# Weight splits, the turned keys' copies and the end of a feed-forward in another order, in a two-block float32 transformer on one core

## The reference, cut

```python
u = a * jax.nn.sigmoid(b)                 # first mixer: conformer branch
u = causal_depthwise_conv(u, w_dw)        # 31 taps, 256 channels
u = jax.nn.silu(layer_norm(u, ln_g, ln_b)) @ w_pw
log_f = jax.nn.log_sigmoid(f_logit)       # first mixer: forgetting attention
...
q = (rms_norm_2(c_q, q_norm) @ w_uq)      # attention: 8 latent heads of 64 + 32 (rope)
kv = (rms_norm_2(c_kv, kv_norm) @ w_ukv)
o_mla = causal_attention(q_mla, k_mla, v_mla, (MLA_NOPE + MLA_ROPE) ** -0.5)
o_diff = o2[:, 0] - lam * o2[:, 1]        # and 4 heads as differences of two maps
...
x = x + (jax.nn.silu(h @ w_gate) * (h @ w_up)) @ w_down
```

## Time and profile before

| what | us |
|---|---|
| median of three runs (1029.54 to 1032.91) | 1031.27 |
| the profiled execution, its own time | 1029.98 |
| its span | 1028.2 |
| TensorE busy | 964.4 (94%) |
| VectorE busy | 705.0 (69%) |
| ScalarE busy | 505.8 (49%) |
| GpSimd busy | 63.7 (6%) |
| chain that ended last: TensorE, VectorE, ScalarE, issue, transfers | 73%, 15%, 5%, 4%, 2% |
| TensorE's granted clock, mean | 0.981 |

### The profile page before, as it was taken

The page is one execution under the profiler, slowest core; times in us unless marked ns, Lnnn a source line. Parts: engine busy times, 40 slices in busy tenths (PEclk is TensorE's granted clock), DMA queues, the critical chain, the costliest instruction groups (busy, mean ns, idle before and its releaser), DMA issues.

```text
span 1028.2 us, 13523 instructions
## 1 busy us (share of the span) xinstructions
PE 964.4 (94%) x5540; PEld 842.5 (82%) x5540; DVE 705.0 (69%) x943; ACT 505.8 (49%) x674; POOL 63.7 (6%) x89
## 2 busy tenths in 40 slices
PE   5989899999999899779999999989999899999997
PEld 5878697888887689667988888868989789888886
DVE  4699576666667786765676666656979776766664
ACT  4755554444436636555544344347655354443441
POOL 4200000000000100000000000010113100000000
PEclk9989999999999999979999999999999999999999
DMA  9554337466464344221566556556331346565531
GB/s 321 187 164 123 123 114 245 164 202 208 164 205 152 128 152 153 83 72 52 166 221 226 178 191 203 166 157 192 123 124 42 123 149 202 183 200 177 197 123 42
DMA packets 106190, 164.40 MB, mean 160 GB/s; under 512 B 2816, under 2 KB 82784, under 8 KB 106000
## 3 DMA queue, kind: packets, MB, share of 16 engines
q1 hardware_dynamic: 104688, 158.25, 46.7%
q0 software_dynamic: 1440, 5.28, 1.5%
HBM read 162.47 MB, written 1.05 MB: 159 GB/s over the span
## 4 chain that ended last, share of the span: by engine, by line
PE 73%; DVE 15%; ACT 5%; issue 4%; DMA 2%; POOL 0%; DVEq 0%; POOLq 0%; ACTq 0%
PE ps L380 71%; DVE wl L1673 6%; PE ps L388 2%; ACT wh L1117 2%; DVE SC L1774 2%; DMA raw<-in_w_in 1%; DVE xhl L1678 1%; DVE xf L1682 1%; ACT junk L1105 1%; ACT SC L1427 1%; DVE st L2078 1%; DVE rows L2277 0%; DMA h<-in_x 0%; DVE hs L2288 0%; POOL st L2434 0%
## 5 line engine op out<-in xcount | busy, mean ns | idle before, releaser
L1673 DVE TENSOR_TENSOR wl<-raw,wh 128x2048 fp32r<-128x2048 f32 (+2 forms) x150 | 339.3, 2264 | 172.0 <-ACT wh L1117 171.8
L1117 ACT ACTIVATE wh<-raw 128x2048 fp32r<-128x2048 f32 (+2 forms) x150 | 282.1, 1885 | 171.4 <-PE ps L380 148.5
L380 PE MATMUL ps<-xhl,wh 128*128 128x512 f32 (+1 forms) x1248 | 281.6, 352 | 4.4 <-DVE wl L1786 4.4
L380 PE MATMUL ps<-wh,xhl 128*128 128x512 f32 (+3 forms) x1000 | 255.5, 347 | 23.9 <-DVE wl L1673 12.1
L380 PEld LDWEIGHTS ps<-xhl,wh 128*128 128x128 f32 x1248 | 216.2, 191 | 31.9 <-issue 5.6
L380 PEld LDWEIGHTS ps<-wh,xhl 128*128 128x128 f32 x1000 | 174.4, 194 | 46.5 <-DVE wl L1673 14.1
L380 PE MATMUL ps<-xhl,wl 128*128 128x256 f32 x1008 | 175.6, 283 | 0.0
L380 PE MATMUL ps<-wl,xhl 128*128 128x512 f32 (+3 forms) x500 | 171.0, 342 | 0.0
L380 PEld LDWEIGHTS ps<-xhl,wl 128*128 128x128 f32 x1008 | 151.5, 191 | 7.5
L380 PE MATMUL ps<-wh,fh 128*128 128x512 f32 x304 | 119.0, 391 | 1.8 <-DVE fl L1924 1.5
L380 PE MATMUL ps<-wh,fl 128*128 128x512 f32 x304 | 118.7, 390 | 0.0
(11 more groups left out here) (266 smaller groups left out, 829.6 us busy)
## 6 DMA issues: line engine op xcount, KB each, us to landing
raw<-in_ffn_gate SPq DMA_DIRECT2D x22, 1024.0 KB, 5.2
raw<-in_ffn_up SPq DMA_DIRECT2D x22, 1024.0 KB, 5.2
raw<-in_ffn_down SPq DMA_DIRECT2D x22, 1024.0 KB, 4.9
raw<-in_w_up SPq DMA_DIRECT2D x16, 1024.0 KB, 5.5
raw<-in_w_down SPq DMA_DIRECT2D x16, 1024.0 KB, 4.8
raw<-in_s_w_in SPq DMA_DIRECT2D x14, 1024.0 KB, 5.3
raw<-in_w_in SPq DMA_DIRECT2D x9, 1024.0 KB, 7.1
raw<-in_a_w_in SPq DMA_DIRECT2D x6, 1024.0 KB, 5.1
```

The lines of the kernel that those rows point to most:

```text
L380: return e.matmul(o, a, b, start=start, stop=stop, skip_group_check=True)
L1117: e.activation(high_of(i), raw_of(i), ACT.Copy).then_inc(*up("act_high", i))
L1673: e.tensor_tensor(low_of(i), raw_of(i), high_of(i).bitcast(F32), ALU.subtract).then_inc(*up("dve_lo", i))
```

## The change

- **First mixer.** Slot a's three products are made one after the other over both column blocks, high by high first, and go to two banks. The gate product becomes two. Slot 5 is split right behind it, before the softplus, and slots 6 to 8 one place further on; the taps lie between them in other numbers (2, 8, 7, 6, 8 for 5, 6, 6, 6, 6, 2 of the first half). The low half of the last output part, `mix_low(3)`, moves ahead of a row maximum, slot 12's split behind the squares. In both softpluses of the kernel the reciprocal of 1+u is made by ScalarE as exp(-log(1+u)).
- **Attention.** Step 4 stands ahead of all ropes on VectorE; `ukv` waits per token half. VectorE copies the turned keys, ScalarE the turned queries. The splits of `aout` move: on ScalarE to steps 5 (two), 8 and 11 from 6, 9, 11 and 18; on VectorE to steps 5, 7, 9 and 17 from 6, 9, 12 and 18.
- **End of f0.** The second token half goes block by block, `norm_turn` stands before its second block, and each `down` slot is released by its block. The splits of `hi` move forward.

Cut to its core (line numbers left out):

```diff
@@ tensor, first_mixer
-                e.wait_ge(*at("dve_xl", 0, 1, 1))
+                e.wait_ge(*at("act_xh", 0, 1, 1))
                 wH, wL = weight(S["a"])
-                for t in range(2):
-                    e.wait_ge(*(halves_ready(S["a"]) if t else at("dve_first_low")))
...
+                for n, (w, x) in enumerate(((wH, xh), (wH, xl), (wL, xh))):
+                    for t in range(2):
...
+                        for k in range(8):
+                            d = mm(ps[(4, 2)[t]][:, 0:256], w[:, k, 128 * t:128 * t + 128], x[:, k, :], n == 0 and k == 0,
+                                   n == 2 and k == 7)
@@ tensor, ffn
-                        if l == "f0" and (tb, half, j) == (1, 1, n - 1):
-                            norm_turn(s_next, 0)
...
+                def down_end_blocks():
+
+                    for j in range(n - 3, n):
+                        wH, wL = weight(down[j])
+                        if j == n - 2:
+                            norm_turn(s_next, 0)
+                        for half in range(2):
+                            for k in range(2):
+                                c = slice(256 * k + 128, 256 * k + 256)
+                                d = mm3(ps[ACC[s_next][1][half]][:, :], fh[:, j % 3, c], fl[:, j % 3, c], wH[:, k, HALF[half]],
+                                        wL[:, k, HALF[half]], False, j == n - 1 and k == 1)
+                            if (j, half) == (n - 1, 0):
+                                d.then_inc(*up("pe_sums", s_next, 1, 0))
+                        d.then_inc(*up("pe_slot", down[j]))
@@ tensor, attention
-                e.wait_ge(*at("dve_rope_read", "q", 1, 0))
-                for tb in range(2):
+                for tb in range(2):
+                    e.wait_ge(*at("dve_rope_read", "q", tb, 0))
@@ scalar, softplus
                 e.activation(l, w, ACT.Ln).then_inc(*up("act_softplus", who, "log"))
+                e.wait_ge(*at("act_softplus", who, "log"))
+                e.wait_ge(*at("dve_softplus", who, "kept"))
+                e.activation(w, l, ACT.Exp, scale=-1.0).then_inc(*up("act_softplus", who, "inverse"))
@@ scalar, first_mixer
                 e.activation(sg, ps[5][:, :], ACT.Sigmoid).then_inc(*up("act_sigmoid"))
+                highs(5)
                 for k in range(5):
                     tap(k)
                 R = slice(0, 36)
                 softplus("forget", *(ft[R, i, :] for i in range(4)), junk[R, 0:256])
-                highs(5)
+                highs(6)
@@ scalar, attention
                         e.activation(o[:, :, 0:64], v[:, :, 0:64], ACT.Copy).then_inc(*up("act_q_latent", i, tb))
+                    if i == 1:
+                        highs(S["aout"][3])
                     tick(4 + i, do)
...
-                highs(S["aout"][2])
                 for c in range(2):
-                    for j, o in enumerate((qT, kT2)):
-                        for tb in range(2):
...
+                    for tb in range(2):
+                        e.wait_ge(*at("pe_qk_turned", 0, tb, c))
+                        e.activation(qT[0:96, 4 * c:4 * c + 4, tokens(tb)],
+                                     ps[(0, 4)[tb]][0:96, :].rearrange("p (k n) -> p k n", k=4),
+                                     ACT.Copy).then_inc(*up("act_q_turned", tb, c))
...
-                    if t == 9:
-                        highs(S["aout"][3])
+                    if t == 8:
+                        highs(S["aout"][0])
                     if t == 11:
-                        highs(S["aout"][0])
+                        highs(S["aout"][1])
@@ scalar, between
                 norm_high(5, 0)
+                highs(S["hi"][0])
                 norm_squares(5, 1)
@@ vector, softplus
-                e.wait_ge(*at("act_softplus", who, "log"))
-                e.reciprocal(w, w).then_inc(*up("dve_softplus", who, "inverse"))
-                e.wait_ge(*at("dve_softplus", who, "inverse"))
+                e.wait_ge(*at("dve_softplus", who, "lost"))
+                e.wait_ge(*at("act_softplus", who, "inverse"))
@@ vector, first_mixer
-                e.tensor_tensor(upad[:, :, 30:286], ps[4][:, :].rearrange("p (t n) -> p t n", t=2),
-                                sg.rearrange("p (t n) -> p t n", t=2), ALU.mult).then_inc(*up("dve_glu"))
-                taps(0, 0, 5)
+                for t in (1, 0):
+                    e.tensor_tensor(upad[:, t, 30:286], ps[(4, 2)[t]][:, 0:256], sg[:, 256 * t:256 * t + 256], ALU.mult).then_inc(
+                        *up("dve_glu", t))
+                lows(5)
+                taps(0, 0, 2)
...
                 lows(11)
+                mix_low(3)
                 forget_max(2)
                 taps(1, 20, 24)
                 forget_inverse(2)
-                mix_low(3)
...
                 e.tensor_tensor(csq, cacc, cacc, ALU.mult).then_inc(*up("dve_conf_square"))
+                lows(12)
@@ vector, attention
                 tick(3, do)
+                tick(4, do)
                 for i in range(2):
...
-                    tick(4 + i, do)
+                tick(5, do)
+                lows(S["aout"][2])
...
+                def keys_turned(c):
+                    for tb in range(2):
+                        e.wait_ge(*at("pe_qk_turned", 1, tb, c))
+                        e.tensor_copy(kT2[0:96, 4 * c:4 * c + 4, tokens(tb)],
+                                      ps[(7, 6)[tb]][0:96, :].rearrange("p (k n) -> p k n", k=4)).then_inc(
+                            *up("dve_k_turned", tb, c))
+
                 tick(6, do)
-                lows(S["aout"][2])
-                for t in range(7, 16):
+                keys_turned(0)
+                tick(7, do)
+                lows(S["aout"][3])
+                keys_turned(1)
+                for t in range(8, 16):
                     tick(t, do)
                     if t == 9:
-                        lows(S["aout"][3])
-                    if t == 12:
                         lows(S["aout"][0])
...
                 mix_low(0)
+                lows(S["aout"][1])
                 tick(18, do)
-                lows(S["aout"][1])
@@ vector, between
                 residual(5, 1)
+                lows(S["hi"][0])
                 norm_mean(5, 1)
-                lows(S["hi"][0])
+                lows(S["hi"][1])
                 norm_scale(5, 1)
-                lows(S["hi"][1])
```

More of the change, by code:

```diff
@@ L47 @@
                   "act_forget_turned act_forget_out act_conf_std act_conf_silu act_conf_out"),
[L48 removed]
+    "act_attention": ("act_latent act_dq act_dk act_dv act_lambda act_q_latent act_k_latent act_v_latent act_q_turned "
                       "act_exp act_map_turned act_latent_out"),
@@ L492, in first_mixer @@
                 norm_turn(0, 1)
-                e.wait_ge(*at("dve_xl", 0, 1, 1))
+                e.wait_ge(*at("act_xh", 0, 1, 1))
                 wH, wL = weight(S["a"])
-                for t in range(2):
-                    e.wait_ge(*(halves_ready(S["a"]) if t else at("dve_first_low")))
-                    c = slice(128 * t, 128 * t + 128)
-                    for k in range(8):
-                        d = mm3(ps[4][:, 256 * t:256 * t + 256], wH[:, k, c], wL[:, k, c], xh[:, k, :], xl[:, k, :], k == 0, k == 7)
+                for n, (w, x) in enumerate(((wH, xh), (wH, xl), (wL, xh))):
+                    for t in range(2):
+                        if n == 0:
+                            e.wait_ge(*(at("act_high", 0) if t else at("act_first_high")))
+                        elif n == 2:
+                            e.wait_ge(*(halves_ready(S["a"]) if t else at("dve_first_low")))
+                        elif t == 0:
+                            e.wait_ge(*at("dve_xl", 0, 1, 1))
+                        for k in range(8):
+                            d = mm(ps[(4, 2)[t]][:, 0:256], w[:, k, 128 * t:128 * t + 128], x[:, k, :], n == 0 and k == 0,
+                                   n == 2 and k == 7)
                 d.then_inc(*up("pe_slot", S["a"]))
@@ L509, in first_mixer @@
                     tok(S["v"], [(ps[1][:, 256 * tb:256 * tb + 256], slice(0, 256))], tb)
+                e.wait_ge(*at("dve_glu", 1))
                 for tb in range(2):
@@ L518, in first_mixer @@
                     if t == 1:
-                        e.wait_ge(*at("dve_glu"))
+                        e.wait_ge(*at("dve_glu", 0))
                     for i in range(2):
@@ L713, in ffn @@
                         down_block(j - 3, 1)
-                for tb in range(2):
+                for half in range(2):
+                    down_end(0, half)
+                if l == "f0":
+                    down_end_blocks()
+                else:
                     for half in range(2):
-                        down_end(tb, half)
+                        down_end(1, half)
             def gate():
@@ L775, in map_logits @@
                     if i == 8:
-                        e.wait_ge(*at("act_qk_turned", 1, 1, 1))
+                        e.wait_ge(*at("act_q_turned", 1, 1))
```

(15 more changed lines are left out.)

12 lines of the change are left out of this document (2 added, 10 removed).

## The result

The changed kernel takes 1018.11 us (median of 4 runs, 1016.93 to 1018.95) where the kernel before took 1031.39 beside it: a ratio of 0.9871, with a 95% interval from 0.9852 to 0.9891. The profiled execution took 1016.93 us, its span is 1015.1, TensorE's busy time 960.7 us (964.4 before) and its granted clock 0.983 in the mean. The forecast was 1018.

A forecast was written before the change was run, and what follows sets the result against it. TensorE, with 73% of the span, was taken as the bound, gaining only where it stands still or another engine is late. +0.5 - 8.1 - 4.7 = -12.3 from 1029.98 gave 1017.7, kept as 1018; range 1013 to 1024.

The forecast's parts named there:

- First mixer, +0.5: First mixer: the mean starts at 99.75 instead of 99.29, so all behind it is 0.5 us later; bounds -0.3 and +3.5.
- VectorE's way up to the softplus: First mixer: waiting for ScalarE's copy, the moved split and two taps bring VectorE to the softplus at 42.7, 1.5 us later.
- the exponential as far as VectorE goes: First mixer's softplus: ScalarE's exponential with table load, 1.70 us, replaces VectorE's reciprocal, 1.75; with the hand-over nothing is won.
- Up to the end of the taps ... 0.7 back: First mixer: the moved split (2.2) is done, three taps (1.5) remain, so the taps end 0.8 us later, at 99.6.
- The bound of +3.5: First mixer's upper bound: GpSimd slows two splits by 0.8 us each, a lowered clock adds 1.7; as rival, 1021, chance 0.10.
- Attention, -8.1: Attention: shorter TensorE waits give -3.0, -1.8, -2.1 and -1.2 us, together -8.1; bounds -5 and -10.
- Map 8's logits: Attention: these start at 433.1 instead of 436.05, 3.0 us earlier, the 1.8 of the first wait included.
- the later waits: Attention behind map 8: TensorE's waits of 3.53, 2.14 and 1.24 us shrink, giving -1.8, -2.1 and -1.2 us.
- VectorE's idle 4.01 us: Attention: VectorE's pause from 423.85 to 427.86, to be used from its start for a split, a mean and key copies.
- End of f0, -4.7: End of the second feed-forward: 0.7 us from an earlier wide projection, 2.56 from a wait, 1.5 from the clock; bounds -3.5, -5.3.
- The third-last block's slot is freed 2.7 us earlier: End of f0: ScalarE copies the third wide slot sooner, VectorE's split ends at 682.1, and TensorE's 2.56 us wait goes.
- the 4.38 us taken for twelve products: End of f0: twelve matmuls behind the 2.56 us wait, at the lowered clock, would take 2.87 us instead; gain 1.5.

The follow-up runs named there:

- the last kernel: Against the kernel before: early reciprocal in the old mixer order, attention's new order with key copies on ScalarE, f0's new end; 1013.67 us, ratio 0.9836.

## Why the prediction was right, step by step

- **First mixer, +0.5: too small.** The mixer's end moved by +1.4 in the pair of traces, by +1.75 over five and five. VectorE's way up to the softplus was right (42.76, forecast 42.7), and so was the exponential as far as VectorE goes. What failed is "Up to the end of the taps ... 0.7 back. The end of the taps moves by +1.5 - 0.7 = +0.8": the taps were priced at their undisturbed length. The end of the taps moved by +1.7 (98.78 to 100.45). The exponential and slot 6's copy put GpSimd's second group beside the first two of eight taps, 0.83 us; the rest is the forecast's 0.8. Taking GpSimd away gave 0.85 back at the mixer's end. The bound of +3.5 held GpSimd's cost, at the wrong operation: I had put it on splits, and they were not slowed (2.29 at 38.78, 2.28 at 55.07). With the rule of the Trainium skill, "SBUF — State Buffer" (Who interferes with whom), that whichever engine starts first holds the shared ports to its end, this agrees: GpSimd's four additions, the first of them begun behind the split, took 4.68 us instead of 3.64. The other rule, of "ScalarE: Activation LUTs" (What ACT_TABLE_LOAD costs), would have put a drain of about 1.38 us behind the load; the operation started 1.30 us after the load did (47.15 and 48.45), so again none shows.
- **Attention, -8.1: right, -8.4 in the pair.** Over three traces with the old attention (87.7 in the mean) and seven with the new one and VectorE's copies (77.8) it is -9.9, so that the forecast is 1.8 short, and the good match in the pair is in part luck: its old trace is the shortest of the three. Map 8's logits came 2.7 earlier (forecast 3.0; -3.4 over all), and a key copy took 0.64 (estimate 0.65). Behind map 8 the gain is 5.7 in the pair and 6.5 over all, for 5.1, but not as summed, wait for wait. TensorE's standing time there fell from 7.29 us to 5.30 only, and its busy time from 43.02 to 39.32, at a clock of 0.87 before and 0.95 after. Nor is the gain the clock's. In six of the seven traces this stretch took 44.62 to 44.71 us at mean clocks from 0.86 to 0.96, with TensorE standing 2.9 to 5.9 us: what TensorE won by its clock it mostly stood, behind VectorE and ScalarE. The old order took 50.31 to 51.49 at 0.87 and 0.88. The clock is not without weight: with the keys on ScalarE the stretch took 43.15 at 1.00 and, in the last kernel, 44.62 at 0.89. Rows of windows from map 8's logits to the last turn, the changed kernel and the one without the mixer's part:

```profile
434.15:478.77 44.62, 39.32 (x224) 32.47 (x225) 27.94 (x94) 25.94 (x81) 2.65 (x4) 0.95 0.22 71
```

```profile
432.43:477.14 44.71, 41.80 (x225) 35.19 (x225) 27.97 (x94) 25.98 (x81) 2.65 (x4) 0.86 0.22 71
```

That the later waits come from the splits' places was shown by putting them back (attention 85.73). But VectorE's copies were no part of the gain: on ScalarE attention is 3.4 us shorter, or 2.1 with the clock of the last kernel. The forecast counted VectorE's idle 4.01 us as free and did not ask whether, with the new order of splits, ScalarE was still late.
- **End of f0, -4.7: right in size, -5.0, wrong in one step.** "The third-last block's slot is freed 2.7 us earlier ... So the 2.56 wait is gone": it is gone without that too. The earlier turn and the splits' new places on both engines carry 3.0; the release by blocks is worth 2.0, 1.4 of it by clearing ScalarE's way to the normed columns. In the sum the 4.38 us taken for twelve products run 0.16 into the turn that begins at 692.45. How the 3.0 divide between turn and splits was not tried.
- **The sum.** By rows +1.75 - 9.9 - 5.0 = -13.2; the times say -13.3. The mixer's error of 1.2 and attention's of 1.8 went opposite ways, so that the closeness of the total, 1018 for 1018.11, is in part luck.

## What to carry to other kernels

Before an engine's idle time is filled with work taken from another, look whether the reordering alone already frees the other: here the splits' places brought attention's gain and the copies moved to VectorE gave 2 to 3 us of it away. Price a step on VectorE by what GpSimd does beside it at its new time, and follow the operation that feeds GpSimd: 1.8 us more on ScalarE moved it onto the taps, and later an earlier reciprocal moved the taps onto it. Compare lengths of stretches over several traces, never absolute times of two.

## What the runs showed that I had not expected

- The same code between mixer and attention took 276.0 to 278.7 us in 14 traces, while f0's end repeats within 0.3 us for each order (220.67 to 220.95, 215.63 to 215.73).
- Waits of nearly one length leave the clock up or down: behind 1.28 us before the mean it was 1.00 in one kernel and 0.52 in another, behind 2.52 us in attention 1.00 and behind 2.30 us 0.50. An earlier mean bought nothing where it fell. What decides it these runs do not show.
